# 64-slot experts' steps mixed into 128-slot experts' steps, and expert weight tiles split whole, in a two-layer model with a mixture of experts

## The reference

```python
N_EXPERTS = 8
TOP_K = 2
EXPERT_DIM = 3584

def moe_swiglu(h, w_router, w_gate, w_up, w_down):
    logits = (h @ w_router).astype(jnp.float32)
    top_val, top_idx = lax.top_k(logits, TOP_K)
    top_w = jax.nn.softmax(top_val, axis=-1)
    gates = jnp.sum(jax.nn.one_hot(top_idx, N_EXPERTS, dtype=jnp.float32) * top_w[..., None], axis=-2)
    out = jnp.zeros_like(h)
    for e in range(N_EXPERTS):
        y = swiglu(h, w_gate[e], w_up[e], w_down[e])
        out = out + gates[..., e:e + 1].astype(h.dtype) * y
    return out
```

## Time and profile before

| | us |
|---|---|
| median of 3 runs (2052.95 to 2055.52) | 2054.3 |
| the profiled execution's own time | 2052.51 |
| its span in the profile | 2050.7 |
| TensorE busy | 2000.7 |
| VectorE busy | 1407.4 |
| ScalarE busy | 1226.2 |
| mean granted TensorE clock (share of full speed) | 0.996 |

### The profile page before, as it was taken

One profiled execution on the slowest core, in us unless ns is written; L12 is line 12 of the kernel. 1 busy time (PEld: TensorE's weight loads), 2 busy tenths in 40 slices (PEclk: granted clock), 3 DMA queues, 4 the chain that ended last, 5 costly groups with the idle time before them and its releaser, 6 DMA issues.

```text
span 2050.7 us, 26538 instructions
## 1 busy us (share of the span) xinstructions
PE 2000.7 (98%) x9924; PEld 1577.5 (77%) x9925; DVE 1407.4 (69%) x2087; ACT 1226.2 (60%) x1911; POOL 70.6 (3%) x92
## 2 busy tenths in 40 slices
PE   9999999999999999889999999779999999999998
PEld 7788888878888886458888887348777788877787
DVE  5665556889999895049999895136665876666676
ACT  6564446667777774047787774035556655455664
POOL 0000000033000000000000000000110000020000
PEclk9999999999999999999999999999999999999999
DMA  7355554279999999999999999985444355544342
GB/s 281 134 203 215 190 191 150 83 282 386 368 381 362 376 371 363 422 421 406 375 380 371 351 372 353 420 331 192 169 153 146 142 172 183 187 156 152 138 157 108
DMA packets 79463, 543.13 MB, mean 265 GB/s; under 512 B 11147, under 2 KB 11403, under 8 KB 14688
## 3 DMA queue, kind: packets, MB, share of 16 engines
q1 hardware_dynamic: 78240, 539.40, 69.1%
q0 software_dynamic: 944, 1.86, 0.2%
q10 hardware_dynamic: 144, 0.10, 0.0%
HBM read 536.32 MB, written 6.55 MB: 265 GB/s over the span
## 4 chain that ended last, share of the span: by engine, by line
PE 90%; DMA 6%; ACT 2%; DVE 2%; issue 1%; ACTq 0%; SPq 0%; DVEq 0%
PE bank L248 26%; PE bank L250 26%; PE bank L249 25%; PE bank L812 4%; DMA ring<-in_moe_tiles 4%; PE bank L2067 2%; DMA moe_ring<-in_moe_tiles 2%; PE bank L2077 1%; DMA ring<-in_hy_tiles 1%; PE bank L3001 1%; PE bank L494 0%; DVE w_low L226 0%; PE bank L3023 0%; DVE w_low L223 0%; PE bank L1992 0%
## 5 line engine op out<-in xcount | busy, mean ns | idle before, releaser
L248 PE MATMUL bank<-w_high,xT_high 128*128 128x512 f32 x1072 | 426.9, 398 | 1.5 <-DVE w_low L223 0.9
L250 PE MATMUL bank<-w_high,xT_low 128*128 128x512 f32 x1072 | 418.4, 390 | 0.0
L249 PE MATMUL bank<-w_low,xT_high 128*128 128x512 f32 x1072 | 417.7, 390 | 0.0
L223 DVE TENSOR_TENSOR w_low<-ring,w_high 128x1024 fp32r<-128x1024 f32 x210 | 258.9, 1233 | 183.9 <-ACT w_high L215 179.9
L215 ACT ACTIVATE w_high<-ring 128x1024 fp32r<-128x1024 f32 x210 | 222.1, 1057 | 205.2 <-PE bank L250 189.9
L248 PE MATMUL bank<-w_high,moe_x_high 128*128 128x512 f32 x672 | 269.6, 401 | 0.0
L250 PE MATMUL bank<-w_high,moe_x_low 128*128 128x512 f32 x672 | 262.9, 391 | 0.0
L249 PE MATMUL bank<-w_low,moe_x_high 128*128 128x512 f32 x672 | 262.2, 390 | 0.0
L226 DVE TENSOR_TENSOR w_low<-ring,w_high 128x1024 fp32r<-128x1024 f32 x210 | 258.1, 1229 | 0.1
L248 PEld LDWEIGHTS bank<-w_high,xT_high 128*128 128x128 f32 x1072 | 201.4, 188 | 44.9 <-issue 4.8
L250 PEld LDWEIGHTS bank<-w_high,xT_low 128*128 128x128 f32 x1072 | 201.2, 188 | 43.1
(11 more groups left out here) (423 smaller groups left out, 3102.5 us busy)
## 6 DMA issues: line engine op xcount, KB each, us to landing
moe_ring<-in_moe_tiles SPq DMA_DIRECT2D x144, 1024.0 KB, 6.9
ring<-in_hy_tiles SPq DMA_DIRECT2D x103, 1024.0 KB, 4.8
ring<-in_moe_tiles SPq DMA_DIRECT2D x96, 1024.0 KB, 6.8
ring_wide<-in_moe_tiles SPq DMA_DIRECT2D x96, 1024.0 KB, 6.9
ring<-in_ffn_tiles SPq DMA_DIRECT2D x17, 1024.0 KB, 4.8
ring_wide<-in_ffn_tiles SPq DMA_DIRECT2D x16, 1024.0 KB, 4.7
ring_wide<-in_gla_in_tiles SPq DMA_DIRECT2D x6, 1024.0 KB, 9.9
ring<-in_sb_in_tiles SPq DMA_DIRECT2D x6, 1024.0 KB, 4.7
```

The costliest lines, as they stand in the source:

```text
L223: self.nc.vector.tensor_tensor(self.low[:, place, FIRST], memory[:, FIRST], self.high[:, place, FIRST].bitcast(F32), ALU.subtract).then_in ...
L248: nc.tensor.matmul(out, x[0], w[0], start=start, stop=False, **more)
L249: nc.tensor.matmul(out, x[0], w[1], start=False, stop=False, **more)
L250: return nc.tensor.matmul(out, x[1], w[0], start=False, stop=stop, **more)
```

## The change

Two edits. First, `NARROW` becomes (2, 4) and `RANK_AT` changes with it, so the narrow experts now belong to rounds two and three, where they are the second of the round (q = 1) in `Round`, and round four has two 128-slot experts. In rounds two and three the steps of both experts are mixed: the first 24 steps (`FEW_BY`) hold all 14 narrow ones and 10 wide ones, as W N W N W N N W N W N N W N W N W N N W N W N N, and the last 4 are wide. Transfers follow the same order. Since both experts are now in work at once, the narrow one's down sums lie in bank 3, and each has a gate column of its own.

Second, each expert tile that is split is rounded in one instruction of 2048 columns (L238 after) and subtracted in one (L243 after), except for the first three tiles of the MoE and those of the next layer; TensorE then waits for the whole tile.

```diff
-RANK_AT = (2, 1, 3, 4, 5, 0)
-NARROW = (3, 7)
+RANK_AT = (1, 2, 0, 3, 4, 5)
+NARROW = (2, 4)
+FEW_BY = 24
...
+    def round_whole(self, act, place, memory, landed, value, before):
+
+        act.wait_ge(landed, value)
+        act.wait_ge(self.used, before)
+        self.nc.scalar.activation(self.high[:, place, :], memory, ACT.Copy).then_inc(self.rounded, 1)
+
+    def rest_of_whole(self, dve, place, memory, rounded):
+
+        dve.wait_ge(self.rounded, rounded)
+        self.nc.vector.tensor_tensor(self.low[:, place, :], memory, self.high[:, place, :].bitcast(F32), ALU.subtract).then_inc(self.split, 1)
...
+class Round:
+
+
+    def __init__(self, few=False):
+        N = MOE_STEPS
+        self.few = few
+        if few:
+            done = [i * N // FEW_BY for i in range(FEW_BY + 1)]
+            kinds = [done[i + 1] - done[i] for i in range(FEW_BY)] + [0] * (2 * N - FEW_BY)
+            self.seq = [(kind, sum(k == kind for k in kinds[:i])) for i, kind in enumerate(kinds)]
+        else:
+            self.seq = [(i // N, i % N) for i in range(2 * N)]
+        self.at = {step: i for i, step in enumerate(self.seq)}
+        self.last = [self.at[q, N - 1] for q in range(2)]
+        self.second = 0 if few else 1
...
                     if k % 2 == 0:
-                        pe.wait_ge(F.split if k else F.split_first, G.splits(n, at - G.first))
+                        pe.wait_ge(F.split if k or G.whole(n, at - G.first) else F.split_first, G.splits(n, at - G.first))
...
             for s in range(STEPS):
-                if s == N + 1:
-                    finished(0)
+                q, c = r.seq[s]
+                for done in range(2):
+                    if s == r.last[done] + 2:
+                        finished(done)
                 if s:
                     turned(s - 1)
```

More of the change, by code:

```diff
@@ L793, in added, with block_half @@
     return lambda n, t: ((K.evac_dve if t else K.evac_act).sem, base[t] + n + 1)
-def block_half(nc, bank, lhs, W, place, t, half, pe, number, turned=None, closed=False):
+def block_half(nc, bank, lhs, W, place, t, half, pe, number, turned=None, closed=False, halves=None):
     for k in range(4):
@@ L801, in block_half @@
         if t == 0 and k % 2 == 0:
-            pe.wait_ge(W.split if k else W.split_first, W.splits(number))
+            if k:
+                pe.wait_ge(W.split, W.splits(number))
+            else:
+                pe.wait_ge(W.split_first, halves or W.halves(W.splits(number)))
         kk = 4 * half + k
@@ L1929, in moe, with narrow_tile @@
         hT_few = K.row_last[:, KC * FEW:KC * FEW + 2 * P].rearrange("p (s n) -> p s n", s=2)
-        narrow_tile = lambda n, u: u < PER and 2 * n + order[u][1] // N in NARROW
+        plain = Round()
+        rounds = [Round(2 * n in NARROW) for n in range(PAIRS)]
+        over_tile = lambda n, u: (n + u // PER, u % PER)
+        def narrow_tile(n, u):
+            n, u = over_tile(n, u)
+            return n < PAIRS and rounds[n].narrow(order[u][1])
         split_tiles, last_at, made_splits, made_free = 0, {}, {}, {}
@@ L1986, in gather @@
             for g, b in enumerate(GATHERED):
+                if g == 1 and before.few:
+                    pe.wait_ge(G.ya, 2 * before.place(n - 1, 1) + 2)
                 if g == 3 and turned is not None:
@@ L2050, in moe, with pe_run @@
         PUT_AT = 6
-        def pe_run(pe, G, n, pair, first_step, late, put=(False, False), narrow=(False, False)):
+        def pe_run(pe, G, n, pair, first_step, late, put=(False, False), r=plain):
             F = G.stream
@@ L2166, in split @@
             def split(u):
-                if u + SPLIT < last_tile and not (any(narrow) and narrow_tile(n, u + SPLIT)):
+                if u + SPLIT < last_tile and not G.unsplit(n, u + SPLIT):
                     round_tile(act, G, n, u + SPLIT)
@@ L2446, in _ @@
                             (lambda: next_sel(dve, pair + 1)) if more else lambda: None,
-                            (lambda: gathered_dve(dve, G, pair + 1, any(is_narrow(pair + 1)))) if more else None, put=is_put(pair), narrow=is_narrow(pair),
+                            (lambda: gathered_dve(dve, G, pair + 1, rounds[pair + 1].few)) if more else None, put=is_put(pair), r=rounds[pair],
                             rows_in={3: lambda: rows_and_gates(dve)} if pair == 0 else {} if more else add_at(dve))
```

175 lines of the change are left out of this document (89 added, 86 removed).

## The result

The changed kernel takes 2036.5 us (median of 4 runs, 2035.03 to 2037.39), the kernel before 2053.6 beside it (2052.95 to 2055.52): 0.9914 of it, with an interval of 0.9897 to 0.9932. The prediction was 2034, with a range of 2022 to 2052. The profiled execution took 2037.34 in its own time, its span is 2035.2.

A forecast was written before the change was run, and what follows sets the result against it. TensorE bounds the kernel, with transfer waits in narrow halves. Round two to the next layer's turns falls from 689.6 to 213.6 x 2 + 239.2 + 3.5 = 669.9; with 0.9, 20.6 us less: 2034 us, range 2022 to 2052.

The forecast's parts named there:

- Rival 3: Mixed rounds: transfers run slower when mixed, 2.8 us a tile, step 24 22 us later, 2078 us; chance 0.03.
- rival 5: Expert places: an expert with more than 64 rows meets a 64-slot place; a further pass, tens of us; chance 0.03.
- 4.8 of waits: Mixed round: behind two narrow steps TensorE waits 1.2 us for the whole tile, 4 times a round.
- The transfers' path: Mixed round: step 24's first tile lands 167.8 us after the round's start, is ready 4.4 later, so step 24 starts at 172.2.
- 4.6 us lost on meeting narrow tiles: Wide-to-narrow border: transfers below full rate because narrow tiles free ring slots only after use; 4.6 us lost.
- rival 2: Mixed rounds stay bound by transfers: some 11 us more a round, 2056 us, half of it 2045; chance 0.18.
- On neither path is more than a microsecond gained by mending the other: Mixed round: TensorE and transfers both reach step 24 at 172.2 us, so mending one gains at most a microsecond.
- Round four and the end: All-wide round four without waiting takes 239.2 us; from the last down to the next layer's turns 3.5 us.
- for disturbances: Round four: additions to h in wide steps cost about 0.5 us of wait in four steps, 2 us; bounds 0 and 5.5.
- the 0.9 us for the clock: Next layer's first microseconds: the lowered granted clock goes, 0.9 us gained.
- Rival 4: Wide steps: whole tiles come too late despite 0.6 us to spare; at 0.6 us of wait 2072 us; chance 0.11.
- Rival 1: Mixed rounds: waits go almost entirely, 208.8 us a round, 2024 us, down to 2018 if changing kinds is free; chance 0.16.

The follow-up runs named there:

- unmixed: The changed kernel with 14 wide, then 14 narrow steps in rounds two and three, whole tiles kept: 2052.5 us; the same with tiles in halves: 2048.0 us.
- half_bytes_halves: The changed kernel with every expert tile split in two halves and only the first half of each narrow tile transferred: 2015.3 us.
- half_bytes: The changed kernel with only the first 1024 of 2048 columns of every narrow tile transferred, whole tiles kept: 2030.6 us.
- halves: The changed kernel with every expert tile split in two halves again, the mixing kept: 2028.8 us.

## Why the prediction was right, and where its terms were off

**The bound was read rightly.** TensorE's waits in the narrow halves were the transfers', and taking them out gave most of what was gained. The unmixed kernels keep the narrow steps of 7.46 us and most of the time with them; 19 of the 25 us gained by mixing and moving are the mixing's. Rival 3 (slower transfers when mixed) fell at 421 GB/s over 156 us, rival 5 (a further pass) with the count of matmuls, 9924 as before.

**A mixed round: predicted 213.6, measured 216.0 and 215.0.** The prediction put two paths at 213.6 each.
TensorE's was predicted 208.8 without waits and 4.8 of waits. Measured 206.9 (half_bytes_halves), 1.9 less. Only 0.4 of that lies in the 24 steps (167.0, not 167.4); the rest of the round took 39.9 and not 41.4, since the 5.8 us of what a round has beside its steps were put behind step 24 whole, while the two row-and-gate groups of matmuls (0.46 and 0.53 us) stand within the 24 steps. With the whole tiles 212.0 and 212.9, so they cost 5.1 and 5.9, near the 4.8, and step 24 began at 172.2 (half_bytes), as predicted. But the cost is differently composed: the four waits are 0.99 three times and 0.45 once, 3.4 us in all and not 4 x 1.2. The tile was ready 6.8 us into the second narrow step, as worked out, but TensorE wanted it at 5.8 and not at 5.6. The rest is hiddenT_low behind a whole subtraction and steps a few tenths longer.

The transfers' path was too short. Its step that failed is "4.6 us lost on meeting narrow tiles", taken from one border of the kernel before: at this one 7.9 us were lost. That the slots come free slower while wide and narrow steps alternate is the likely reason, which no run here takes apart. Step 24 began at 859.39 - 683.26 = 176.1 and not at 172.2. Its first tile landed at about 854.9, an estimate: ScalarE waited for no transfer at 855.02, and the tile behind it landed at 857.42, 2.485 later. That is 171.7 us into the round where 167.8 had been predicted, and 3.3 of the 3.9 are the larger loss. Behind it the 4.4 us of a whole tile came as worked out. That is rival 2 in its mechanism (the mixed rounds bound by transfers) at a small part of its price.

The 2.4 us by which round two missed are 3.9 too few up to step 24 and 1.5 too many behind it; that these went against each other was luck.

**"On neither path is more than a microsecond gained by mending the other"** was wrong. Taking out the splits' waits gave 2.5 and 1.4 us a round, taking out the transfers' 4.0 and 2.2. The reason, as far as the traces of round two show it: the paths are no two sums compared at the round's end. TensorE's last wait for a late tile ended at 849.62 in the changed kernel and 846.26 with halves, 166.4 and 164.6 us into the round, where transfers set the pace. ScalarE could begin that tile at 161.7 and 160.8 (844.99 and 842.42), 1.0 of the 1.8 between them; the other 0.8 is its way through the two engines. A late tile is through ScalarE and VectorE up to hiddenT_low in 4.15 us when whole (776.86 to 781.01), in 3.37 by halves (775.32 to 778.69). Then the pair before step 24 adds its 0.99 in the changed kernel and nothing with halves. 1.8 and 1.0 are the 2.5, to 0.3. For round three this wasn't followed step by step.

**Round four and the end: predicted 239.2 + 3.5 = 242.7, measured 242.0.** The whole tiles cost 2.6 here (halves 239.4), where the prediction had 2 "for disturbances". These 2 are 0.5 in each of the four steps with additions to h; the additions cost 0.5 in all, in steps of 8.60, 8.48, 8.61 and 8.47 us in place of 8.41. The larger losses are one step of 9.46 us, three steps after the last expert's first, where ScalarE's sum of its gates (L2269) waits for VectorE's selection rows (L2348) and the next whole tile stands behind it, and the last step, as TensorE's timeline of the changed kernel shows:

```profile
1264.73 0.47 PE L264 MATMUL bank<-w_high,moe_x_high 128*128 128x512 f32 x1 [0.80 <-DVE w_low L243]
...
1349.09 0.44 PE L831 MATMUL bank<-consts_sb,moe_hidden 128*128 128x128 f32 x2 [0.83 <-DVE moe_hidden L2328]
```

In the last step silu's product stands behind a whole subtraction. The end took 2.6 from the last down's end where 3.5 had been predicted, and the 0.9 us for the clock came: from the turns to the span's end 678.95 us, before 679.95. No row that the prediction shows gave that term; the traces have it. The granted clock is 0.85 from 1370.75 to 1380 before, and 1.00 from 1356.25 to 1366 after.

**Rival 4, the other side.** The slack of 0.6 us was real: steps in pure wide stretches last 8.41 to 8.42 us with whole tiles as with halves. It is used up wherever something else comes: 0.6 within round one's first two steps, and 0.24 at each of the two places where a step takes 8.92 us for its row and gate (the kernel with halves has the 8.92 as well, without the 0.24). Round one became 1.1 us longer than before; I had costed it at nothing.

**The sum.** Of the 5.4 us by which the profiled execution is above the 2031.9 worked out for it, the mixed rounds are 3.8, round four with the end -0.7, round one 1.1, and the rest is ahead of the MoE (1.0, which the kernels' traces scatter by anyway, 439.8 to 440.9 at the MoE's first matmul) and outside the span (0.3). That the median is only 2.5 above the 2034 is in part luck: the prediction put the median 1.8 above the profiled execution, as it stood before, and after the change it stands 0.9 below.

**Two small slips in the working.** ScalarE's fit gives 1.95 us for a whole tile, not 1.93 (measured 1.91). Rival 1's lower end of 2018 is short of its own terms: 19 changes of kind at 0.26 are 4.9 us a round, which gives 2014.

**The instruction counts.** VectorE has 2087 - 1839 = 248 instructions fewer, and a whole tile saves 2 x 1225 - 2291 = 159 ns there and 2 x 1055 - 1912 = 198 ns on ScalarE. Neither engine is the bound, so nothing came of it, while the consumer lost the head start of a first half.

## What to carry to other kernels

When one kind of step starves for data and another has bandwidth to spare, alternate them on the scale of the buffer's lead, spread to the very end of the round, and don't leave the starved kind last: here that gave 19 us of 2054 for the mixing, 3 to 4 for the last two steps of spread, and 6 for keeping narrow steps out of the last round. Merging a producer's two instructions into one saves its fixed cost but takes the head start from whoever consumes the first half; if the producer isn't the bound and its slack is tenths of a microsecond, keep the halves (here they were worth 4.5 to 7.7 us). When two paths come out level on paper, don't expect their maximum: their waits stand at different steps, and a part of them adds up (here 5.1 and 6.6 us alone, 9.1 together).

## What the runs showed of the hardware

The transfers of this single core ran at 421 GB/s for 156 us without a break, with wide and narrow tiles mixed, at a DMA share of 1.01. The Trainium skill, "Perfetto Trace Analysis", section Roofline, says that 358 GB/s is a core's share when both cores of a pair work, and that one alone may go to about 435; with that the trace agrees, and it is the reading to take of the figure that the prediction weighed.

The granted clock is 0.98 in the narrow half of before, where TensorE waited for each tile, 0.99 in the unmixed rounds, and 1.00 in the mixed ones, whose waits are shorter. The down that ends round two took 3.55 us behind a wait of 3.88, and 3.29 behind a wait of 3.50 in the run unmixed, where 1.9 is usual. The windows of these two, before and then unmixed, show why:

```profile
899.18:902.66 3.48, 3.48 (x9) 0.84 (x9) 3.48 (x5) 1.75 (x2) 0.00 (x0) 0.53 1.01 421
901.20:904.42 3.22, 3.22 (x8) 0.79 (x8) 3.11 (x6) 1.64 (x1) 0.00 (x0) 0.57 1.02 425
```

The mean granted clock is 0.53 and 0.57 there, most of it at the lower of its two levels (1.2 of 2.4 GHz). In the mixed rounds, with waits of 1.9 us at most (halves), the mean stays at 1.00.
